# Moving the last sixteen rounds of block-sum gathers on GpSimd from one stage of a decoder step to the next

## What is computed

```python
h = rmsnorm(x); u, v, z_a, p, z_b = split(h @ w_in_even)          # even layer
x = x + concat(gmlp(u, v) * silu(z_a), pool(p) * silu(z_b)) @ w_out_even
h = rmsnorm(x); q, kc, vc, ks, vs, kw, vw, g, z = split(h @ w_in_odd)   # odd layer
q = rope(rmsnorm(q)); k_ = rope(rmsnorm(k_))                      # 16 query heads, 4 key heads, 3 branches
means = blocks_of_64(concat(cache_cmp[page_table], kv_cmp)).mean()      # compressed branch
x = x + (attention(q, k, v, means, gates) * silu(z)) @ w_out_odd
```

## Time and profile before

| | us |
|---|---|
| median of 3 runs | 2330.07 |
| lowest and highest run | 2328.7 and 2333.64 |
| the profiled execution, its time | 2340.24 |
| the profiled execution, its span | 2338.7 |
| TensorE busy in the span | 2117.5 (91%) |
| VectorE, ScalarE, POOL busy | 793.9, 670.9, 639.6 |
| POOL in the 128 gathers (line 1901) | 230.8, and 215.4 idle before them |

### The profile page before, as it was taken

One profiled execution on the slowest core, in us unless ns is written; L12 is line 12 of the kernel. 1 busy time (PEld: TensorE's weight loads), 2 busy tenths in 40 slices (PEclk: granted clock), 3 DMA queues, 4 the chain that ended last, 5 costly groups with the idle time before them and its releaser, 6 DMA issues.

```text
span 2338.7 us, 47836 instructions
## 1 busy us (share of the span) xinstructions
PE 2117.5 (91%) x17058; PEld 1915.8 (82%) x17058; DVE 793.9 (34%) x1140; ACT 670.9 (29%) x1063; POOL 639.6 (27%) x711
## 2 busy tenths in 40 slices
PE   5799999999999799999999999958777688888999
PEld 4799999999999799999999999945554355446999
DVE  1533332424322532232232311123332356555221
ACT  3322122222322222222223222234434145444221
POOL 3253544444443242344255500011322100000000
PEclk8899999999999999999999999969988799999999
DMA  8388897978988745554323344177888300003442
GB/s 248 84 190 179 181 190 156 201 171 183 216 214 208 200 128 178 166 163 133 100 73 90 94 115 113 49 251 256 293 285 272 121 28 13 23 23 91 136 135 78
DMA packets 348648, 352.37 MB, mean 151 GB/s; under 512 B 15065, under 2 KB 286610, under 8 KB 347762
## 3 DMA queue, kind: packets, MB, share of 16 engines
q1 hardware_dynamic: 298978, 213.85, 31.5%
q0 software_dynamic: 38560, 128.54, 23.6%
q10 hardware_dynamic: 11008, 8.52, 1.1%
HBM read 327.31 MB, written 40.76 MB: 157 GB/s over the span
## 4 chain that ended last, share of the span: by engine, by line
PE 75%; DMA 7%; issue 7%; DVE 5%; POOL 3%; ACT 1%; SPq 1%; DVEq 1%; POOLq 0%; ACTq 0%
PE main L358 52%; PE main L639 4%; DMA block_sum<-cache_cmp_kv,block_row 3%; PE aux L1020 3%; PE aux L911 2%; PE main L1062 2%; DMA sel_k<-cache_sel_kv 2%; PE main L1086 2%; PE main L959 1%; PE aux L605 1%; PE aux L923 1%; PE aux L780 1%; POOL v_norm L1927 1%; DVE act_lo L592 1%; DMA win_v<-win_kv_sample_out 1%
## 5 line engine op out<-in xcount | busy, mean ns | idle before, releaser
L358 PE MATMUL main<-act_hi,w_hi 128*128 128x260 f32 x3808 | 777.8, 285 | 7.0 <-DVE w_lo L348 7.0
L358 PE MATMUL main<-act_hi,w_lo 128*128 128x260 f32 x3808 | 768.5, 283 | 0.0
L358 PE MATMUL main<-act_lo,w_hi 128*128 128x260 f32 x3808 | 767.1, 283 | 0.0
L358 PEld LDWEIGHTS main<-act_hi,w_hi 128*128 128x128 f32 x3808 | 589.3, 189 | 8.8 <-issue 7.4
L358 PEld LDWEIGHTS main<-act_hi,w_lo 128*128 128x128 f32 x3808 | 588.1, 189 | 0.0
L358 PEld LDWEIGHTS main<-act_lo,w_hi 128*128 128x128 f32 x3808 | 587.7, 189 | 0.0
L348 DVE TENSOR_TENSOR w_lo<-w_raw,w_hi 128x2048 fp32r<-128x2048 f32 x129 | 295.5, 2291 | 384.1 <-ACT w_hi L343 380.2
L1901 POOL DMA_INDIRECT block_sum<-cache_cmp_kv,block_row x128 | 230.8, 1803 | 215.4 <-DMA block_sum<-cache_cmp_kv,block_row 198.7
L343 ACT CAST w_hi<-w_raw 128x2048 fp32r<-128x2048 f32 x129 | 246.1, 1908 | 56.8 <-issue 23.1
L2024 POOL DMA_DIRECT2D sel_v<-cache_sel_kv x120 | 64.6, 538 | 412.5 <-issue 288.6
L1305 ACT COPY sel_k_t<-aux 128x512 f32<-128x512 f32 x160 | 88.8, 586 | 143.2 <-PE aux L911 143.0
(11 more groups left out here) (283 smaller groups left out, 2036.8 us busy)
## 6 DMA issues: line engine op xcount, KB each, us to landing
w_raw<-w_in_odd SPq DMA_DIRECT2D x56, 1024.0 KB, 5.6
w_raw<-w_in_even SPq DMA_DIRECT2D x40, 1024.0 KB, 6.0
sel_k<-cache_sel_kv SPq DMA_DIRECT2D x128, 256.0 KB, 5.4
sel_v<-cache_sel_kv POOLq DMA_DIRECT2D x120, 256.0 KB, 4.1
w_raw<-w_out_even SPq DMA_DIRECT2D x16, 1024.0 KB, 12.6
w_raw<-w_out_odd SPq DMA_DIRECT2D x16, 1024.0 KB, 7.2
win_kv_sample_out<-state_win_kv SPq DMA_DIRECT2D x8, 2044.0 KB, 10.2
win_k<-win_kv_sample_out SPq DMA_DIRECT2D x8, 1024.0 KB
```

Source lines behind the costliest of these rows:

```text
L358: ins = nc.tensor.matmul(MP[:, slot, b, 0:HALF], w_[:, slot, k, :], x_[:, k, b * HALF:(b + 1) * HALF], start=(k == 0 and q == 0), stop=(k ...
```

## The change

The two gathers of a round are no longer issued behind each store of x in the first layer's output tiles. They are issued behind the two stores of the three key tiles and of the first value tile (c < 4) of each pass of the second layer's key and value loop, as round 48 + 4 i + c. For this the loop over the four passes is written out in Python instead of run by the hardware, so that the round, the column and the semaphore values are constants there. Nothing is computed otherwise than before.

```diff
@@ -1944,7 +1944,6 @@
                 slot = kt % 2
                 pool.wait_ge(evac[slot], (N_EVEN_OUT + kt) // 2 + 2)
                 nc.gpsimd.dma_start(x1_scr[kt], A[:, kt, :]).then_inc(sem("x1_out"), 16)
-                add_rows(48 + kt)
 
 
             pool.wait_ge(sem("y_used"), 9)
@@ -1986,7 +1985,7 @@
                 pseq2.do(nc.gpsimd.tensor_tensor(x2, RA[:, :, 16:32], RB[:, :, 16:32], ALU.add))
                 pool.sem_inc(sem("rows_ready"), 1)
 
-            with pool.Fori(0, KV) as i:
+            for i in range(KV):
                 pseq2.loop(i, 8 * 3, 8)
                 for c, (kind, col0, br) in enumerate(KVT):
                     slot = c % 2
@@ -1995,12 +1994,14 @@
                         rotate(6 * i + c, 3 * i + c, slot, 1 + br)
                     else:
                         wait(pool, sem("rows_read"), 6 * i + c + 2)
-                    col = nc.gpsimd.snap((0 if c < 3 else 512) + i * P, min_val=0, max_val=1024 - P)
+                    col = (0 if c < 3 else 512) + i * P
                     nc.gpsimd.dma_start(kv_p[br].rearrange("(j p) c -> p j c", p=P)[:, :, bass.ds(col, P)],
                                         KN[:, slot, 0:TT, :]).then_inc(sem(f"rows_out{slot}"), 16)
                     dst = kv_s[br] if br < 2 else kv_s[2][:, 511, :]
                     nc.gpsimd.dma_start(dst[:, bass.ds(col, P)], KN[0:NS, slot, 4, :]).then_inc(
                         sem(f"rows_out{slot}"), 16)
+                    if c < 4:
+                        add_rows(48 + 4 * i + c)
             with pool.Fori(0, KV) as i:
                 pseq2.loop(i, 8 * 4, 104)
                 for e in range(REP):
```

## The result

| | before | after |
|---|---|---|
| median, us | 2330.27 (4 runs) | 2349.65 (4 runs) |
| lowest and highest | 2328.70 and 2333.64 | 2346.92 and 2352.88 |
| profiled execution, span | 2340.24, 2338.7 | 2346.92, 2345.3 |
| key and value loop, first main product to the first product behind the loop | 318.0 | 332.5 |
| TensorE's wait for POOL in the loop | 0.3 | 13.8 |

The change makes the kernel slower: 1.0082 [1.0063, 1.0100], that is 19.4 us (14.7 to 23.3). The forecast was 2336 with a range up to 2346: the sign was right, the size was about a third of what came. Stages can.

What follows compares the result with a forecast made beforehand. TensorE was taken to bound the kernel, with POOL's keys due at deadlines with 0.46 to 1.13 us slack. Stalls of about 1.5 us a pass over four passes made 6 us, forecast 2336 us on the runs' scale, range 2329.5 to 2346.

Steps and rivals of the forecast that it cites:

- The output tiles give nothing: First layer's output tiles: TensorE is busy throughout and waits for nobody, so losing two gathers per tile gains 0.
- transfers cost nothing: Output tiles: DMA engines get freer, but weights are already in time, 0; key 0 and key 1 pairs: no landing wait, 0.
- the fourth pair: Behind each pass's first value tile: POOL stands about 6 us for an earlier gather's landing, but nothing of TensorE's queues behind.
- the last pass's later stores: Last pass: stores behind the gathers delay VectorE's split of the second query tile; priced at 0, 2 us kept for range.
- VectorE's lock: Key and value loop: w_lo under one pair per pass on the way to key 2 adds 2.1 us x 4 = 8 us, 2344.
- rival 3: The pair is longer where it now stands, by VectorE's lock (2344) or by TensorE's clock (2348); chance together 0.08.
- says why: Claim that the skill explains long gathers: VectorE holding the shared port pair keeps GpSimd from writing DMA descriptors.
- the key's length of 8.53: POOL's time for key 1 in the second pass, down from 9.40: eight gaps shrinking by 0.11 save about 0.87 us.
- the prediction's sum: Second pass of the loop: TensorE stalls 0.1 us for key 1 and 1.35 for key 2; about 1.5 a pass, 6 us.
- rival 2: Key and value loop: writing-out saves little, as waits for other engines' semaphores set a key's pace; 2341 to 2353, chance 0.15.
- The clock: Key and value loop: TensorE's product after a stall runs slow, 2.9 us; in each pass 12 us, 2348.
- upper bound for the sum: Key and value loop: unrolling gives nothing, stalls of 2.8 and 2.9 us, 5.7 x 4 = 23 us, 2353.

## Why the prediction was right in direction and wrong in size

**What held.** The output tiles give nothing (the window of the earlier trace rows had left out the first tile, which the experiment without the rounds covers), transfers cost nothing, the fourth pair and the last pass's later stores cost nothing (the product of 23.03 us behind the loop stands unbroken at 1133.76). The gaps between POOL's dependent steps fell from 0.18 to 0.07. The pairs landed on the path where the prediction had them, the waits are those of key 1 and key 2, and the pass got longer by idle time. That VectorE's lock would lengthen a pair on this path (half of rival 3) didn't happen: the pairs between keys took 1.70 to 1.72 and 1.56 to 1.57 us, at one place 1.58. In the third pair, off the path, it did; POOL's row and VectorE's:

```profile
963.22 3.00 POOL L1901 DMA_INDIRECT block_sum<-cache_cmp_kv,block_row  x1 [0.30 <-issue]
```

```profile
962.49 2.29 DVE L348 TENSOR_TENSOR w_lo<-w_raw,w_hi 128x2048 fp32r<-128x2048 f32 x1 [4.43 <-ACT w_hi L343]
```

The gather ends 1.44 us after the low half. The Trainium skill (SBUF — State Buffer, section "SBUF: two separate sides") has such a lock for VectorE operations in a 2-port mode, and for those with two inputs in SBUF only against a GpSimd operation that reads SBUF. The low half is a TENSOR_TENSOR with two inputs in SBUF, so the prediction's "says why" went further than the section: the rows show that the gather is held up, and no run here shows whether it is its descriptors or its row numbers that wait.

**The step that failed** is the length of a hop, that is "Its two stores now begin after 0.30 instead of 0.85 us and take about 1.25", together with the key's length of 8.53. In the second pass:

| from key 0's first step to key 1's last | predicted | measured | late by |
|---|---|---|---|
| key 0 | 8.58 | 8.79 | 0.21 |
| gap before the stores | 0.30 | 0.61 | 0.31 |
| two stores | 1.25 | 1.44 | 0.19 |
| pair with its issue | 3.75 | 3.9 | 0.15 |
| key 1 | 8.53 | 8.68 | 0.15 |

Key 1 is 1.0 us later than worked out, and, since the next hop has the same errors, key 2 is 1.9 us later. All the slack was already spent in the prediction's sum, so every tenth of this went into the stall: 1.5 us a pass became 3.45 (13.8 through four), 6 us became 13.8. The store terms came from the wrong row. I took the first layer's store of the sample rows as the stand-in for the stores of the loop, because it was issued with constants; but the loop's own prompt store, at 0.84 us in the earlier trace rows, measures the operation itself, and constants leave that duration as it was (0.84 in the loop written out alone, 0.89 in the changed kernel). Only the gap ahead of it shrinks, from 0.84 to 0.61, not to 0.30; why it stays twice the first layer's 0.30 no run shows. The key lost 0.66 to 0.72 us, not 0.87: seven gaps between POOL's own steps, not eight, at a tenth each.

So rival 2, "the writing-out saves little", has the result in its 2341 to 2353, and half of its reason: between one key's start and the next key's the writing-out saved some 0.9 us (0.7 in the key, 0.2 around the stores), where the prediction had counted 1.6. But the gaps did shrink, and no wait for another engine set POOL's pace between the keys except the one for VectorE's scaling, 1.05 us a key, which was in the sum.

**The clock** was the other half of rival 3, at a chance of 0.08 for both halves: priced at 2.9 us in each pass, it came once in the loop, at 1.5. The price was one draw: the product that the earlier trace rows has at 14.46 us took 11.77 in two other kernels behind the same wait. By itself it would not have moved the result out of the range.

**The sum as it should have been:** the two waits of a pass and the longer turn-backs, four times 3.6 or 14.4 with the small savings of the written-out passes, and the slow product 1.5: 15.9, against 19.4 (14.7 to 23.3) and 17.2 (12.8 to 21.7) measured in the two sets of runs. The remaining 1 to 4 us lie within the intervals and no stage shows them.

**The range** failed for a reason of its own. Its upper bound for the sum was 23 us, from an unrolling that gives nothing, and the result lies below that; but I left the upper half of it to two rivals of 0.15 and 0.08 and cut the range at 2346. The sum was a small difference (1.5) between lengths of 13 to 14 us, each with errors of tenths, and such a difference deserved the bounds' full width.

## What to carry to other kernels

Work that is queued on an in-order engine ahead of a step with a deadline is free up to the slack; beyond that, each hop costs what the engine's pitch exceeds that of the engine that waits (14.8 less 12.5 us here, not the 3.9 of the pair). So compare the engine's whole pitch from one such step to the next with the pitch of the engine that waits, rather than adding up savings and costs at one deadline. Take the duration of an operation from the row of that very operation, even in the loop that is to be rewritten, before a similar one elsewhere. And first ask what the stage that loses the work could give back: leaving the work out altogether answers it in one run.

## What the runs showed of the hardware

- In the written-out loop, behind the stores of key 0 or key 1, the first accumulating gather held POOL 1.70 to 1.73 us (1.60 behind the single store of the earlier trace rows) and the second 1.56 to 1.58; 0.30 us of issue goes ahead of each, and POOL's next arithmetic step begins 0.08 us after the last one's end, although in the loop of the changed kernel a gather lands 7.0 us (median) after its issue. The Trainium skill (Perfetto Trace Analysis, section "DMA Instruction — SWDGE (GPSIMD)") says that the profile ends such an instruction when its descriptors are made, not when its data has moved; the rows agree.
- A gather issued while VectorE makes the low half of a weight tile ended 1.41 to 1.44 us after VectorE's operation, however early it was issued: so in ten cases from four kernels, with lengths of 2.04 to 3.64 us.
- A store issued behind a dependent POOL step came 0.61 to 0.65 us after it at nine of twelve places of the changed kernel's loop, with constant addresses, and 0.75 to 0.95 at three; one arithmetic step follows another after 0.07 to 0.08.
- None of twenty waits of 1.17 to 1.84 us ahead of a turn-back lowered TensorE's granted clock. Of eight of 1.95 to 2.06 us, in two executions of the changed kernel, two did, both in the third pass, and each cost 1.5 us. A wait of 2.7 to 2.75 us ahead of the loop's second product cost that product 0.2 us in two kernels, 1.5 to 1.7 in four and 2.9 in four; one of 3.52 us ahead of the output tiles cost nothing in two. So the length of a wait doesn't decide it alone, and what else does no run here shows.
